# A two-layer hybrid decoder trunk on one core: twelve tiles of layer 0's output projection dealt out anew over four head steps

## What is computed

```python
def _even_mixer(h, w_in, b_f, sinks, w_out, rel_bias):
    proj = h @ w_in
    qa, ka, va, fa, qb, kb, vb = _split(proj, EVEN_SIZES)
    F = jnp.cumsum(jax.nn.log_sigmoid(fa + b_f), axis=1)
    out_a = _blocked_causal_attn(qa, ka, va, F)                     # 8 heads of 64
    out_b = _swa_with_sinks(qb, kb, vb, sinks, rel_bias[:, :N_B])   # 8 heads of 64, window 128
    return jnp.concatenate([out_a, out_b], axis=-1) @ w_out         # 512x1024 @ 1024x1024
...
x = x + _even_mixer(_rmsnorm(x, norm_mix_e[e]), w_in_e[e], ...)
x = x + _mlp(_rmsnorm(x, norm_mlp[i]), w_mlp1[i], w_mlp2[i])        # squared ReLU, 4096 wide
```

## Time and profile before

| | |
|---|---|
| median of three runs | 1174.38 us |
| the profiled execution's own time | 1174.1 us |
| its span | 1172.2 us |
| TensorE busy (share of the span) | 1138.0 us (97%) |
| VectorE, ScalarE, GpSimd busy | 813.6, 587.9, 441.3 us |
| mean granted TensorE clock | 0.994 |
| HBM traffic over the span | 92 GB/s |

### The profile page before, as it was taken

One profiled execution on the slowest core, in us unless ns is written; L12 is line 12 of the kernel. 1 busy time (PEld: TensorE's weight loads), 2 busy tenths in 40 slices (PEclk: granted clock), 3 DMA queues, 4 the chain that ended last, 5 costly groups with the idle time before them and its releaser, 6 DMA issues.

```text
span 1172.2 us, 17232 instructions
## 1 busy us (share of the span) xinstructions
PE 1138.0 (97%) x6469; PEld 976.3 (83%) x6469; DVE 813.6 (69%) x1358; ACT 587.9 (50%) x1042; POOL 441.3 (38%) x344
## 2 busy tenths in 40 slices
PE   7999999999999999999999899999999999999997
PEld 5788887788989989988867688888889899899886
DVE  5866787679678668444669898746896686674433
ACT  6677677455354354124465387854543443442333
POOL 2434333451141141157744374445411401511552
PEclk9999999999999999999999999999999999999999
DMA  5242431441421431143322000205415224311332
GB/s 164 76 112 80 119 113 46 145 126 54 171 81 52 164 88 55 36 136 106 91 73 73 19 1 28 82 19 180 126 41 176 74 70 145 89 55 37 106 90 90
DMA packets 154378, 105.16 MB, mean 90 GB/s; under 512 B 9062, under 2 KB 138385, under 8 KB 154306
## 3 DMA queue, kind: packets, MB, share of 16 engines
q1 hardware_dynamic: 153036, 104.09, 29.5%
q10 hardware_dynamic: 1270, 0.13, 0.1%
HBM read 102.04 MB, written 6.35 MB: 92 GB/s over the span
## 4 chain that ended last, share of the span: by engine, by line
PE 81%; DVE 10%; ACT 4%; issue 3%; POOL 1%; DMA 1%; SPq 0%; DVEq 0%; ACTq 0%; POOLq 0%
PE bank L789 25%; PE bank L791 24%; PE bank L790 24%; PE bank L993 2%; PE bank L995 1%; ACT probs L1534 1%; DVE probT_l L1979 1%; DVE score L2410 1%; PE bank L1005 1%; POOL wl L1792 1%; PE bank L1006 1%; ACT ur L1297 1%; DVE best L2406 1%; DVE bank L2289 1%; ACT wh L1297 1%
## 5 line engine op out<-in xcount | busy, mean ns | idle before, releaser
L1792 POOL TENSOR_TENSOR wl<-raw,wh 128x512 fp32r<-128x512 f32 x245 | 340.2, 1412 | 615.4 <-ACT wh L1297 596.3
L789 PE MATMUL bank<-ur,wh 128*128 128x512 f32 (+1 forms) x784 | 296.7, 378 | 1.1 <-POOL wl L1792 0.9
L791 PE MATMUL bank<-ur,wl 128*128 128x512 f32 (+1 forms) x784 | 295.0, 376 | 0.0
L790 PE MATMUL bank<-ur,wh 128*128 128x512 f32 x688 | 267.9, 389 | 0.0
L1297 ACT ACTIVATE wh<-raw 128x1024 fp32r<-128x1024 f32 x123 | 129.0, 1054 | 226.5 <-PE bank L791 226.4
L789 PEld LDWEIGHTS bank<-ur,wh 128*128 128x128 f32 x784 | 147.6, 188 | 30.3 <-issue 4.1
L791 PEld LDWEIGHTS bank<-ur,wl 128*128 128x128 f32 x784 | 147.6, 188 | 27.0
L790 PEld LDWEIGHTS bank<-ur,wh 128*128 128x128 f32 x688 | 129.2, 188 | 26.6 <-issue 0.5
L790 PE MATMUL bank<-xhl,wh 128*128 128x512 f32 (+2 forms) x392 | 143.2, 365 | 0.0
L789 PE MATMUL bank<-xhl,wh 128*128 128x512 f32 (+1 forms) x296 | 120.7, 408 | 4.6 <-DVE xhl L2049 3.0
L791 PE MATMUL bank<-xhl,wl 128*128 128x512 f32 (+1 forms) x296 | 116.0, 392 | 0.0
(11 more groups left out here) (259 smaller groups left out, 2240.5 us busy)
## 6 DMA issues: line engine op xcount, KB each, us to landing
raw<-in_w_mlp SPq DMA_DIRECT2D x80, 512.0 KB, 3.9
raw<-in_w_in_e SPq DMA_DIRECT2D x18, 512.0 KB, 3.6
probs<-in_w_mlp SPq DMA_DIRECT2D x12, 512.0 KB, 4.8
rstd_qk<-in_w_mlp SPq DMA_DIRECT2D x12, 512.0 KB, 4.0
sq<-in_w_mlp SPq DMA_DIRECT2D x12, 512.0 KB, 5.2
raw<-in_w_in_o SPq DMA_DIRECT2D x10, 512.0 KB, 3.8
raw<-in_w_out_e SPq DMA_DIRECT2D x8, 512.0 KB, 4.1
raw<-in_w_out_o SPq DMA_DIRECT2D x8, 512.0 KB, 3.7
```

The costliest lines, as they stand in the source:

```text
L789: mm(dst, lhs[0], rhs[0], start=start, stop=False, skip_group_check=not check)
L790: mm(dst, lhs[0], rhs[1], start=False, stop=False, skip_group_check=not check)
L791: return mm(dst, lhs[1], rhs[0], start=False, stop=stop, skip_group_check=not check)
L1792: return nc.gpsimd.tensor_tensor(dst, a, b, ALU.subtract)
```

## The change

Only the table is changed, in four of its entries. The twelve tiles are the four contraction tiles of the A heads for output tiles 0, 1 and 2. Before, each of the steps 9 to 12 had three of them; after, they have six, two, two and two.

```diff
-OUT_TILES_AT = {9: ((0, 0, 3),), 10: ((0, 3, 4), (1, 0, 2)), 11: ((1, 2, 4), (2, 0, 1)), 12: ((2, 1, 4),),
+OUT_TILES_AT = {9: ((0, 0, 4), (1, 0, 2)), 10: ((1, 2, 4),), 11: ((2, 0, 2),), 12: ((2, 2, 4),),
```

## The result

The changed kernel takes 1179.17 us (median of ten runs, 1177.52 to 1179.68); the kernel before, on the same chip, 1174.30 (ten runs, 1172.50 to 1176.88). The ratio is 1.0039, with a 95% interval of 1.0031 to 1.0048: 3.6 to 5.6 us slower, and just beyond the 0.3% that the prediction called the limit. It is not the ratio of the two medians, which lie 4.87 us apart. Forecast were 1177.9 us, +3.5, with a range of 1175.5 to 1180.3.

The account below looks back on a forecast made before the run. TensorE, busy 97% of the span, was taken as the bound, with steps 9 to 13 turning at VectorE's pace. Waits of 2.09 us plus 1.4 for the clock made 3.5, giving 1177.9 us; range 1175.5 to 1180.3.

Parts of the forecast that it names:

- The first wait: Head of step 9: TensorE idles 3.35 us after scores(11), until GpSimd's subtraction gives the fourth A tile (`att_lo` 4).
- VectorE's cover: Steps 9 to 10: VectorE's other work hides part of 5.2 us; values(10) follow values(9) by 4.94, 2.40 us late.
- The second wait: Start of step 11: TensorE idles some 2.15 us until GpSimd has split the weights of output tile 2.
- The waits' sum: At values(12): both waits together leave them 2.09 us late, with no recovery taken afterwards.
- The clock: Behind step 9's new idle: the low clock falls on tiles and values(9), adding 1.4 us; forecast with this fall only, 0.36.
- the slow stretch of before is in the 189.20: Values(12) start at 189.20 us in the profile before, a moment that already includes step 10's low-clock stretch.
- The row at 13.83: Profile before, another stage: the clock fell after a 2.16 us idle ending at 13.83, cited for a second fall.
- The clock staying up: Rival: the clock stays up at both new idles, or falls only at the second; 2.1 to 3.1 us, chance 0.18.
- both waits bringing it down: Rival: the clock falls behind the idles of steps 9 and 11; 4.5 us, 1178.9, chance 0.28.
- GpSimd's work: Rival: GpSimd's split of tile 2's weights is stretched, 2.0 us more on step 11's wait; 5.5 us, 1179.9, chance 0.05.
- the late start made up: Rival: part of the 2.09 us vanishes in steps 13 to 15 or the projection; 1 to 2 us in all, chance 0.07.
- No-loss: Rival at step 9: GpSimd's subtraction is through well before its row ends, so nothing is late; 1174.4 us, chance 0.06.

Follow-up runs that it names:

- the order experiment: The changed kernel with only step 9's order altered, the tile that needs `att_lo` 4 going last; 1175.36 us, ratio 1.0011 to the kernel before.
- one and five: The kernel before with 1, 5, 3, 3 tiles in steps 9 to 12, two moved from step 9 to step 10; 1174.42 us, ratio 0.9996.
- the repetition: The changed kernel run once more, unaltered, with six runs; 1178.11 us, ratio 1.0037 to the kernel before.

## Why the prediction was right, point by point

*The first wait* was where and what it was said to be: idle of 3.12 to 3.14 us for 3.35 (the release took 0.10 us where I had taken 0.26 from a VectorE release), and the tiles at 4.2 us at the high clock (170.77 to 174.96). By the order experiment it makes 28.94-26.73 = 2.2 us of the loss at values(13).

*VectorE's cover.* Values(9) to values(10) are 4.90 and 4.91 us, for 4.94.

*The second wait* was forecast at 2.15 us and is 2.00; values(11) are 6.30 us behind values(10), for 6.39. Alone, in the order experiment, it leaves 26.73-26.07 = 0.66 us.

*The waits' sum.* 2.09 us against the profile before; measured 28.94-27.15 = 1.79. The difference is nearly all in the two releases, 0.16 and 0.1.

*The clock.* 1.4 us for the fall behind the first idle; measured 1.55. Whether it falls differs from run to run of one kernel, which no row of before could show. Of the five profiles with an idle of 3.12 to 3.14 us ahead of the tiles, two have the fall. The second idle did not bring it down in any of the four profiles that have it. The Trainium skill, in TensorE: Matmul & The Clock Gate, section "Why this matters for your kernels", asks only for gaps between bursts of matmuls to be kept short, and by it a gap of 2.00 us passes at full clock. Those four profiles agree with it; the falls behind 2.82 and 2.16 us do not. The row at 13.83, on which I built the chance of 0.28, is no sure sign either: twelve of the thirteen profiles have an idle of 2.16 or 2.17 us there, and the low level began within 1.7 us of its end in eight and not in four.

*The size.* Of 4.6 us (0.39%) I had 3.5, just below the interval of 3.6 to 5.6. The mechanisms were right; the term that was mis-sized is the clock. The prediction took one execution of each kernel for all: for the kernel before the profiled one, with the fall in step 10 ("the slow stretch of before is in the 189.20"), and for the changed one an execution with the fall behind the first idle. The two first profiles happen to be such a pair, and give 3.34 us at values(13) for the 3.5. Had neither fallen, it would be 28.94-26.07 = 2.87 us; had only the changed kernel's fallen, 4.42. That the forecast was so near is partly luck in which executions were profiled.

The rest of the 4.6 us goes with which low stretches the runs have. Take only runs of equal mean clock, those of the kernel before from the three series of experiments and those of the changed kernel from both its series (not all on one chip). At 0.994 the median spans are 1172.5 (26 runs) and 1175.8 us (4), at 0.992 they are 1174.05 (34) and 1177.5 (9), at 0.997 1170.8 (7) and 1174.2 (1). That is 3.3 to 3.45 us each time, next to the 3.34 of the profiles. And the changed kernel has more runs at the low end: 10 of its 16 had 0.992 or less, and 35 of 86 of the kernel before. Why, stays open. The mean clock does not tell where the low stretches are: of the profiles at 0.994 that of the kernel before has one in step 10, and "one and five" and the order edit have none between 166 and 200 us, but the longer one near 658.

*The rivals.* The clock staying up is what the repetition's profile shows, with 1.79 us at values(13) against the profile before and 1176.0 us in time; both waits bringing it down was seen in no profile. GpSimd's work was not stretched in the changed kernel (2.49 us), nor the late start made up. The Trainium skill, in SBUF — State Buffer, section "Who interferes with whom", says that a VectorE instruction with two inputs in SBUF contends with a GpSimd instruction that reads SBUF; the prediction set this aside for the row. The trace agrees with the page where the split was moved to step 9: there it meets a VectorE subtraction with two inputs in SBUF, and both lose a microsecond. In step 10, where this change leaves the split, each longer VectorE operation beside it takes an input from PSUM, and the split keeps its 2.49 us. No-loss failed on the wait itself: TensorE was not released before the subtraction's row had ended.

## What to carry to other kernels

Before filling work is moved to where an engine idles, look up when each operand is made: a wait at the head of a group holds back all of the group and what stands behind it. Here six tiles with the late one last cost 2.2 us less than the same six with its wait first. In these steps, where VectorE sets the pace, idle of TensorE cost only what it did to the clock and to the work behind it. For effects of 0.3%, compare runs of equal mean clock beside the medians, since one profile shows one draw of the low stretches. And a filler that seems to sit on the path, as the three tiles behind the last head, can be bridging someone else's latency.

## What the runs showed of the hardware

An idle of 3.1 us brought TensorE's clock down to 1.2 GHz in some executions and not in others of the same kernel (3.12 us: down for 3.4 us; 3.14 us in the repetition: not). In the profile with counts 6, 1, 1, 4 it was down for twice that, from 168.9 to 175.7. The idle of 4.1 us near 658 us brought it down in all thirteen profiles, for 3.4 us in four of them and for 6.8 in nine; one of 2.16 us near 13.8 us did so in eight of twelve, and one of 2.00 us in step 11 in none of four. A GpSimd subtraction 128x512 and a VectorE subtraction 64x512 that both read two operands from SBUF held each other up by 1.0 us (two halves each: VectorE 2.38 for 1.39 us, GpSimd 3.46 for 2.49).
